# Two transformer blocks, two layers each, on one core: gather moved behind the gate products, filler matmuls taken from the attention jobs, picks turned in float32r

## The reference, cut to what matters

```python
def hier_moe(x, rg_w, rg_b, re_w, re_b, w_gate, w_up, w_down):
    t = x.reshape(B * S, D)                       # 256 x 1024
    ...                                           # one group of 4 a token, its 2 best experts of 8
    gate = (g_hot[:, :, None] * (p_top * gate_e)[:, None, :]).astype(x.dtype)
    y = jnp.zeros_like(t)
    for g in range(N_GROUPS):
        h = jax.nn.silu(jnp.einsum('td,edf->tef', t, w_gate[g])) * jnp.einsum('td,edf->tef', t, w_up[g])
        y = y + jnp.einsum('tef,efd->td', h * gate[:, g, :, None], w_down[g])
    return y.reshape(B, S, D)
```

## Time and profile before

| | us |
|---|---|
| three runs, median (lowest to highest) | 1759.35 (1757.1 to 1760.42) |
| the profiled execution, its own time | 1757.68 |
| its span | 1755.5 |
| TensorE busy, matmuls | 1726.0 |
| VectorE busy | 866.8 |
| ScalarE busy | 657.7 |

### The profile page before, as it was taken

How to read it: one execution, slowest core, us unless ns; L and a number is a source line. 1 busy time by engine, 2 the same in 40 slices (tenths; PEclk the granted TensorE clock), 3 DMA queues, 4 the chain that set the end, 5 groups by cost and what they waited for, 6 DMA issues and landing times. The chain is left out here.

```text
span 1755.5 us, 24353 instructions
## 1 busy us (share of the span) xinstructions
PE 1726.0 (98%) x9884; PEld 1306.6 (74%) x9884; DVE 866.8 (49%) x1403; ACT 657.7 (37%) x925; POOL 134.4 (8%) x194
## 2 busy tenths in 40 slices
PE   9999999999999999999999999999989999999997
PEld 6888889998988888999889874444459987444442
DVE  6575564444656565444568563222245855332213
ACT  4456353334464634333445421111134452211111
POOL 1020001111112001111111000000001100000000
PEclk9999999999999999999999999999999999999998
DMA  8544455553643454555466068999946605899993
GB/s 305 191 142 146 169 166 180 183 190 132 228 154 134 168 178 165 186 191 167 144 212 186 1 240 354 401 409 416 398 178 203 197 23 223 322 401 405 414 401 134
DMA packets 151677, 396.65 MB, mean 226 GB/s; under 512 B 19984, under 2 KB 84496, under 8 KB 126992
## 3 DMA queue, kind: packets, MB, share of 16 engines
q1 hardware_dynamic: 151568, 395.18, 61.2%
HBM read 394.10 MB, written 1.05 MB: 225 GB/s over the span
## 5 line engine op out<-in xcount | busy, mean ns | idle before, releaser
L815 PE MATMUL ps<-split,split 128*128 128x256 f32 (+3 forms) x1872 | 630.7, 337 | 2.4 <-DVE split L793 0.8
L819 PE MATMUL ps<-split,split 128*128 128x256 f32 (+3 forms) x1872 | 627.8, 335 | 0.6 <-DVE split L2113 0.6
L816 PE MATMUL ps<-split,split 128*128 128x256 f32 (+3 forms) x1872 | 623.4, 333 | 0.0
L793 DVE TENSOR_TENSOR split<-ring,split 128x2048 fp32r<-128x2048 f32 x137 | 314.6, 2303 | 256.1 <-ACT split L786 256.1
L815 PEld LDWEIGHTS ps<-split,split 128*128 128x128 f32 x1872 | 351.5, 188 | 37.5 <-DVE split L808 2.0
L819 PEld LDWEIGHTS ps<-split,split 128*128 128x128 f32 x1872 | 351.7, 188 | 36.8 <-DVE split L2113 2.0
L816 PEld LDWEIGHTS ps<-split,split 128*128 128x128 f32 x1872 | 352.8, 188 | 33.4 <-issue 0.5
L786 ACT ACTIVATE split<-ring 128x2048 fp32r<-128x2048 f32 x137 | 262.1, 1916 | 280.2 <-PE ps L819 272.9
L2707 DVE SCALAR_TENSOR_TENSOR arena<-arena,ps 128x256 f32<-128x256 f32 x32 | 15.4, 481 | 212.9 <-ACT arena L2041 212.9
L808 DVE TENSOR_TENSOR split<-ring,split 128x1536 fp32r<-128x1536 f32 (+3 forms) x44 | 80.7, 1850 | 28.2 <-ACT split L802 28.0
L802 ACT ACTIVATE split<-ring 128x1536 fp32r<-128x1536 f32 (+3 forms) x44 | 67.7, 1546 | 69.9 <-PE ps L819 67.1
(11 more groups left out here) (262 smaller groups left out, 1975.9 us busy)
## 6 DMA issues: line engine op xcount, KB each, us to landing
ring<-in_w_in SPq DMA_DIRECT2D x52, 1024.0 KB, 4.9
ring<-in_w_gate_up SPq DMA_DIRECT2D x44, 1024.0 KB, 5.3
ring<-in_expert_w_gate SPq DMA_DIRECT2D x32, 1024.0 KB, 8.4
ring<-in_expert_w_up SPq DMA_DIRECT2D x32, 1024.0 KB, 10.6
ring<-in_expert_w_down SPq DMA_DIRECT2D x32, 1024.0 KB, 11.4
ring<-in_w_down SPq DMA_DIRECT2D x22, 1024.0 KB, 4.8
ring<-in_w_in SPq DMA_DIRECT2D x28, 768.0 KB, 4.5
high<-in_expert_w_gate SPq DMA_DIRECT2D x16, 1024.0 KB, 7.3
```

What stands on the lines that cost most here:

```text
L793: nc.vector.tensor_tensor(split(slot), slot, split(high[:, n % HIGH, :]), ALU.subtract).then_inc(low_done.sem, 1)
L815: nc.tensor.matmul(acc, sh, mh, start=start, stop=False)
L816: nc.tensor.matmul(acc, *second, start=False, stop=False)
L819: return nc.tensor.matmul(acc, *third, start=False, stop=stop)
```

## The change

1. `gate_up2` no longer gathers. The first gather comes behind it, ahead of the scatter (in pair 0, ahead of `turn_hidden`). ScalarE evicts it after Silu instead of ahead of it.
2. The second gather goes to PSUM bank 3 instead of bank 1. It no longer waits for the eviction of the first. The second half of `down2`, which writes bank 3, waits for the second gather's eviction. `turn_picks`, which writes bank 1, waits for the first gather's eviction.
3. `keep_running` stays ahead of jobs 0 to 2 alone.
4. `turn_picks` multiplies `pick` in float32r with an identity in float32r instead of transposing in float32, and with the gate weights split into a high and a low float32r part (4 columns). VectorE adds the parts when it takes them out. Three VectorE operations ahead of `gate_done` make the identity and the parts.

```diff
-                out += [(("xg", pass_, four, f), 1) for f in (d % 2 * 2, d % 2 * 2 + 1)]
+                out += [(("xg", pass_, four, d % 2 * 2 + f), 1 + 2 * f) for f in range(2)]
...
                     acc = claim2(("S", j, 0), l)
-                    keep_running(acc, 1)
+                    if j < 3:
+                        keep_running(acc, 1)
...
                     acc = claim2(("S", j, part), l)
-                    if part == 0:
-                        keep_running(acc, 1)
...
-                        of = [moe_split(pick[:, t, d * P:(d + 1) * P]).bitcast(F32) for t in range(TT)]
+                        of = [moe_split(pick[:, t, d * P:(d + 1) * P]) for t in range(TT)]
                         for t in range(TT):
-                            nc.tensor.transpose(acc[:, t * P:(t + 1) * P], of[t], ident[:])
-                        gate_ = gate_flat.rearrange("p (t n) -> p t n", t=TT)
-                        for t in range(TT):
-                            mm = nc.tensor.matmul(acc[:, SEQ:SEQ + 2], of[t], gate_[:, t, 2 * d:2 * d + 2],
-                                                  start=(t == 0), stop=(t == TT - 1))
+                            nc.tensor.matmul(acc[:, t * P:(t + 1) * P], of[t], moe_split(ident_moves), start=(t == 0),
+                                             stop=False)
+                            mm = nc.tensor.matmul(acc[:, SEQ:SEQ + 4], of[t], moe_split(gate_parts_flat)[
+                                :, (t * DUOS + d) * 4:(t * DUOS + d + 1) * 4], start=False, stop=(t == TT - 1))
...
-                            if k == KT // 2 and four + 1 < FOURS:
-                                pe.wait_ge(pT_in.sem, pT_in.at(lp, d + 1))
-                                gather(four + 1, 2 * of_four)
...
                         for half in range(2):
+                            if half == 1 and d // 2 + 1 < FOURS:
+                                evicted(d // 2 + 1, 2 * (d % 2) + 1)
...
                         gate_up2(d)
-                        if d == 0:
-                            evicted(1, 0)
-                            gather(1, 1)
-                            turn_hidden(0)
-                        elif four + 1 < FOURS:
-                            scatter(d - 1)
+                        if four + 1 < FOURS:
+                            pe.wait_ge(pT_in.sem, pT_in.at(lp, d + 1))
+                            gather(four + 1, 2 * of_four)
+                            if d > 0:
+                                scatter(d - 1)
                             turn_hidden(d)
-                            evicted(four + 1, 2 * of_four)
                             gather(four + 1, 2 * of_four + 1)
...
-                                evicted(four + 1, 2 * of_four + 1)
+                                evicted(four + 1, 2 * of_four)
...
-                        if four + 1 < FOURS:
-                            gathered(four + 1, 2 * of_four)
                         acc = content_p("gu", d)
                         if d >= 2:
                             act.wait_ge(h2_done.sem, h2_done.at(lp, d - 1))
                         nc.scalar.activation(sg[:, d % 2, :], acc[:, 0:EH], ACT.Silu).then_inc(g2_silu.sem, 1)
+                        if four + 1 < FOURS:
+                            gathered(four + 1, 2 * of_four)
...
+                nc.vector.tensor_copy(moe_split(ident_moves), ident[:])
+                step(nc.vector.tensor_copy(moe_split(gate_parts[:, :, :, 0, :]), gate_pairs))
+                nc.vector.tensor_tensor(moe_split(gate_parts[:, :, :, 1, :]), gate_pairs,
+                                        moe_split(gate_parts[:, :, :, 0, :]), ALU.subtract).then_inc(gate_done.sem, 1)
...
-                            last = nc.vector.tensor_copy(gslot[rows, d:d + 1], acc[rows, SEQ + i:SEQ + i + 1])
+                            last = nc.vector.tensor_reduce(gslot[rows, d:d + 1], acc[rows, SEQ + i:SEQ + i + 3:2], AX_X,
+                                                           ALU.add)
```

More of the change, by code:

```diff
@@ L468, in build @@
         gslot = carve(DUOS)
+        gate_parts_flat = carve(TT * DUOS * 4)
+        gate_parts = gate_parts_flat.rearrange("p (t d s e) -> p t d s e", t=TT, d=DUOS, s=2)
+        ident_moves = carve(P)
         pick_flat = carve(TT * GROUPS * EXPERTS * SLOTS)
@@ L477, in build @@
         earlier_twins = len(twins)
-        twin_of(pick_flat, pickT, Y, H_high)
+        twin_of(gate_parts_flat, ident_moves, pick_flat, pickT, Y, H_high)
         moe_twins = twins[earlier_twins:]
@@ L2655, in _ @@
                 step(last)
-                nc.vector.tensor_tensor(gate, chosen, weight.unsqueeze(2).to_broadcast([P, TT, GROUPS, EXPERTS]),
-                                        ALU.mult).then_inc(gate_done.sem, 1)
+                step(nc.vector.tensor_tensor(gate, chosen, weight.unsqueeze(2).to_broadcast([P, TT, GROUPS, EXPERTS]),
+                                             ALU.mult))
+                gate_pairs = gate_flat.rearrange("p (t d e) -> p t d e", t=TT, d=DUOS)
+                nc.vector.tensor_copy(moe_split(ident_moves), ident[:])
+                step(nc.vector.tensor_copy(moe_split(gate_parts[:, :, :, 0, :]), gate_pairs))
+                nc.vector.tensor_tensor(moe_split(gate_parts[:, :, :, 1, :]), gate_pairs,
+                                        moe_split(gate_parts[:, :, :, 0, :]), ALU.subtract).then_inc(gate_done.sem, 1)
                 def moe_pass(pass_):
```

## The result

| | us |
|---|---|
| before, median of 4 runs (lowest to highest) | 1759.44 (1757.1 to 1760.42) |
| changed, median of 4 runs (lowest to highest) | 1740.12 (1739.59 to 1742.35) |
| ratio, 95% interval | 0.9895 (0.9877 to 0.9912) |
| the changed kernel's profiled execution, its own time | 1742.35 |
| its span | 1738.6 |

What follows compares the result with a forecast made beforehand. TensorE's full queue was taken to bound experts and jobs. A layer's 4.4 + 0.75 + 0 + 2.7 = 7.85 us, 15.7 in two layers, gave 1742.0 against the profiled execution, 1743.5 against the median; range 1738 to 1751.

Steps and rivals of the forecast that it cites:

- The loads' rival: Experts: weight loads set the pace, a 15.4 us pair needing 408 GB/s; price 0 to 4 us, up to 1747; chance 0.05.
- That the jobs wouldn't gain: Attention jobs: ScalarE or VectorE is really the bound, so removing fillers gains nothing; 5.4 us lost, 1749; chance 0.06.
- the clock's fall in the jobs: Attention jobs: without the filler the clock falls to 1.2 GHz; with 20 us a layer the kernel takes 1783; chance 0.06.
- its window of 9.83 us: Stretch 1438.67:1448.50 without filler, only turns and 64-column products, at granted clock 1.00; taken as evidence that the clock holds.
- 0.34 us a pair: Pairs 1 to 13: first gather beside the scatter pays one float32r entry instead of two; 4.4 us a layer.
- its own 0.75 us for pair 0: Pair 0, without scatter: gate and up shorten by 1.30 us, down products start later (2.75 against 2.20); 0.75 us saved a layer.
- plus the extra 0.11 us at entry and 0.09 at exit that the gather shows: Turn of the picks: the gather's surcharges added to four load-paced products, 0.44 us, giving the lower end 0.64 us.
- The slow turn: Rival for the turn of the picks: it costs 0.88 us instead of 0.70, 5.4 us lost, 1749; chance 0.16.
- 13 x 0.215: Attention jobs: thirteen of sixteen fillers a layer removed, each priced from one filler; 2.8 us a layer.
- The wait that the prediction put at 0.15 us for job 3's turn: Attention jobs: three fillers earlier, job 3's turn waits for ScalarE's exponentials, some 0.15 us, leaving 2.7 us a layer.
- job 5's period near 1.6 us: Sign expected in the new trace: job 5 of the attention stage takes near 1.6 us instead of 1.82.
- that part doesn't change: Whole kernel: the profiled execution's time exceeds its span, 1755.5, by 2.2 us, and this stays the same.

Runs made afterwards that it cites:

- the last one above: The changed kernel with the picks turned ahead of the down products, and turned by the old two float32 transposes and two float32 products: 1735.18 us in one run.

## Why the prediction was right, and where it wasn't

**Right in place.** TensorE's queue bounded the experts and the jobs, and what left the queue left the time. The loads' rival falls: pairs of 15.33 and even 14.95 us show no wait for a load. The DMA share of 1.01 stands for a bound at 14.9 us a pair, and the change stayed above it. That the jobs wouldn't gain falls as a whole and came true in one job: job 5 was held up by ScalarE in both layers. So does the clock's fall in the jobs: 1.00 throughout. The prediction read its window of 9.83 us as a third transposes; 20 of the 92 instructions there are. The Trainium skill (TensorE: Matmul & The Clock Gate, Part 4: PE-mode transpose) would have had turns count for less; no window of the jobs here shows a loss by it.

**The gathers.** 0.34 us a pair was forecast, 0.35 came in the whole change and 0.36 alone; pair 0 0.75 against 0.81 (14.75 to 13.94). Together 5.2 forecast a layer and 5.6 measured (13 x 0.365 + 0.81). Bank 3 costs nothing, as forecast. But the prediction gave it no worth, and its own 0.75 us for pair 0 rests on it: with bank 1 pair 0 takes 14.51 us.

**The turn of the picks: the mis-sized term.** Forecast 0.70 us, bounds 0.64 to 0.88, measured 0.53. The failed step is "plus the extra 0.11 us at entry and 0.09 at exit that the gather shows": shown is 0.09 for both. It gives 0.18 x 32 = 5.8 us that the sum lacks. The bound was no bound, since it took the gather's two surcharges as fixed. The slow turn falls with it. The Trainium skill (Perfetto Trace Analysis, Transposes) asks for transposes in place of ordinary matmuls, and the prediction took that as a price; as a price the trace doesn't agree, since a float32 transpose and a float32r product with the identity cost 0.11 us each. No version had both forms in one type, so what the rule is worth at equal types isn't shown.

**The jobs.** Forecast 2.7 us a layer, measured 1.97 and 2.26. "13 x 0.215" failed, since one job's filler was taken for all. Jobs 8 to 14 give back 0.22 us each, jobs 4 and 6 0.16, jobs 3, 5 and 7 together 0.04 in layer 1 and 0.33 in layer 2, and job 15 0.09, having its new wait. In none of the jobs 4 to 14 does the filler's step (0.22, from job 8 on 0.31) come back whole, as a neighbour takes 0.05 to 0.09 us more without it. The wait that the prediction put at 0.15 us for job 3's turn came: the scores' step ahead of it grew by 0.19 us in layer 1 and 0.07 in layer 2 against job 6. So the sign "job 5's period near 1.6 us" was missed (1.90 and 1.78).

**What the sum left out.** With both router stretches undisturbed the spans differ by 1755.5 - 1734.5 = 21.0 us: 16.7 from the experts and 4.2 from the jobs, where 15.7 had been forecast. (A fall of the clock between the two layers, at 1297.4, is in the 1734.5 too and costs it about 0.6 us; the 1755.5 has none.) The router's clock took 4.2 us in the changed kernel's first execution and none in its second, but on the medians it nearly cancels: the spans of the changed kernel's four runs have a median of 1736.5, those of sixteen runs of before 1757.2, each about 2 us above its undisturbed one, and 20.7 apart. What brings these 20.7 to 19.3 is the step "that part doesn't change" of the time beside the span. That part was 2.1 to 2.4 us in every run of before whose span is known, in the version with the gathers alone and in the one without filler; it is 3.4 to 3.8 in all that hold the new float32r buffers, also in the last one above, which has the buffers and not the turn. So 1.3 us go there, and they come with the buffers or the VectorE operations that fill them. Why they do stays open; no version had the one without the other.

The forecast was 3.4 us too high: 5.8 from the turn and 2 x 0.4 from the gathers were not counted, less 1.2 that the jobs didn't give and 1.3 beside the span, makes 4.1. Of the other 0.7 the forecast's own sum explains 0.2 (1742.0 and 1.7 are 1743.7); the rest is within what the router's clock moves from run to run. That the median came so near has luck in it: the turn's error of 5.8 us was partly covered by two of the other sign.

## What to carry to other kernels

Where one engine's queue is full and nothing waits, read start times, take out what stands in the queue, and pay attention to what neighbours what: moving a 0.53 us group of narrow products from between two rows of wide float32 products to behind another float32r group gave 0.37 us a pair, twice what making it cheaper gave (0.18). Then look at what comes next: at 14.95 us a pair the loads, 14.9, are as long as TensorE's work. The best version here is that one, at 1728.3 us against 1759.3. A second bank that is worth nothing in one order (0.8 us a layer) can be what makes the next order possible (1.37 us in each of 28 pairs), so look at the waits of the order you want and not only of the one you have.

A filler's cost read in one job is not the saving in all: look at each kind of job, and at what the engine behind it was waiting for.

Before a difference in one stretch is put down to a change, profile the same kernel once more: the router's 1.3 and 2.9 us had two plausible causes in the program, the missing filler and the moment at which the stretch begins, and the fall came and stayed away with either.

## What the runs showed of the hardware

- float32r products with 128 rows cost 0.11 us each at 4 and at 128 columns, and 0.12 at 256; a 128-column float32 transpose 0.11 too. A separate entry and exit is 0.20 us around a gather (0.11 and 0.09) and 0.09 around four narrow ones.
- The step from the float32 down products to anything small is 0.10 us longer than the step to the float32 gate products (3.58 against 3.48), whether a float32 transpose or a float32r product comes first.
- The granted clock fell to the 1.2 GHz level in 12 of 28 router stretches, for the same kernel in one execution and not in the next; in both layers of the changed kernel TensorE had been busy for 4.8 us or more since a pause of 0.8 us (1030.45 to 1036.4 and 1465.1 to 1469.9), and the execution in which the clock held had the same pause. What decides it is open.
- A wait of 1.09 us cost 1.37.
- One core's loads of 1 MB landed every 2.48 to 2.49 us (421 GB/s) beside full matmul work, in the kernel before and in the fastest version.
- The time beside the span is 2.1 to 2.4 us, and 3.4 to 3.8 in the versions with the new float32r buffers. Why is open.
